# Hybrid encoder, one core: tile 0's index tables per piece, its four pieces routed in one run ahead of the first dots, projections of tiles 1 to 3 behind them

## The reference

```
h = h + even_layer(h)     # attention and a short convolution, joined, then @ even_w_out
h = h + peer_ffn(h)       # first expert block
h = h + odd_layer(h)      # pooling
h = h + peer_ffn(h)       # second expert block

def peer_ffn(x):          # per row; 8 heads, 128 + 128 sub-keys a head, 16 experts kept
    h = rms_norm(x, norm_g)
    q = h @ w_query                                  # 1024 -> 8 heads * 2 * 128
    s = q . sub_keys                                 # 2 lists of 128 scores a head
    sv, si = top_k(s, 16)
    top_s, pos = top_k(all 16 * 16 sums of sv, 16)   # two-step top 16 of 16384 experts
    idx  = expert numbers at pos                     # 128 a row
    gate = softmax(top_s)
    act  = gelu(expert_u[idx] . h)                   # 128 gathered rows of 1024, dotted
    return (gate * act) @ expert_v[idx]              # 128 more gathered rows, summed
```

## Time and profile before

| | |
|---|---|
| runs | 3245.25, 3246.49, 3247.8 us; median 3246.49 |
| the profiled execution | 3245.31 us, span 3243.3 us |
| busy over the span | PE 75%, DVE 69%, POOL 64%, ACT 16% |
| bytes moved | 1134.19 MB, 349 GB/s from HBM over the span |
| gathers | 2080, the first at 498.43 us, the last at 3226.14 us |

### The profile page before, as it was taken

How to read it: one execution, slowest core, us unless ns; L and a number is a source line. 1 busy time by engine, 2 the same in 40 slices (tenths; PEclk the granted TensorE clock), 3 DMA queues, 4 the chain that set the end, 5 groups by cost and what they waited for, 6 DMA issues and landing times.

```text
span 3243.3 us, 28912 instructions
## 1 busy us (share of the span) xinstructions
PE 2422.3 (75%) x5784; PEld 1036.3 (32%) x5784; DVE 2237.6 (69%) x5345; ACT 511.1 (16%) x1370; POOL 2073.7 (64%) x2147
## 2 busy tenths in 40 slices
PE   7999983886777667766678667867776777666667
PEld 3575341332223223322233233323332333222223
DVE  1123187798679866975699668976797679766663
ACT  1026211111111111111111111111111111111111
POOL 0000105777777777766777777777777777777776
PEclk9999996998899989988999899988999899998889
DMA  3121008999999999999999999999999999999999
GB/s 105 52 115 57 30 1 328 400 403 408 409 408 403 394 409 409 408 405 408 409 407 404 404 407 393 401 403 402 404 397 403 399 409 408 407 399 409 409 410 353
DMA packets 319926, 1134.19 MB, mean 350 GB/s; under 512 B 37824, under 2 KB 42944, under 8 KB 317792
## 3 DMA queue, kind: packets, MB, share of 16 engines
q0 software_dynamic: 299520, 1090.65, 85.0%
q1 hardware_dynamic: 20320, 42.62, 3.6%
HBM read 1130.97 MB, written 2.10 MB: 349 GB/s over the span
## 4 chain that ended last, share of the span: by engine, by line
PE 30%; DMA 23%; issue 18%; DVE 18%; POOL 7%; ACT 1%; DVEq 1%; SPq 0%; POOLq 0%; ACTq 0%
DMA v_ring<-in_peer_v,idx_v 18%; PE psum L1319 14%; DMA u_ring<-in_peer_u,idx_u 5%; DVE u_ring L1411 4%; POOL u_ring L1296 4%; PE psum L529 3%; POOL v_ring L1300 3%; PE psum L623 3%; PE psum L957 2%; PE psum L649 2%; DVE hres L1403 2%; PE psum L560 2%; DVE work L1082 1%; PE psum L989 1%; DVE si L1098 1%
## 5 line engine op out<-in xcount | busy, mean ns | idle before, releaser
L1319 PE MATMUL psum<-v_ring,w_col 128*128 128x512 f32 x3136 | 1700.6, 681 | 717.7 <-DMA v_ring<-in_peer_v,idx_v 636.2
L1411 DVE SCALAR_TENSOR_TENSOR u_ring<-u_ring,psum 128x1024 f32<-128x1024 f32 x1040 | 1256.4, 1216 | 541.0 <-DMA u_ring<-in_peer_u,idx_u 501.4
L1296 POOL DMA_INDIRECT u_ring<-in_peer_u,idx_u x1040 | 1018.6, 979 | 496.0 <-issue 264.3
L1300 POOL DMA_INDIRECT v_ring<-in_peer_v,idx_v x1040 | 1039.2, 999 | 318.1 <-issue 276.7
L1319 PEld LDWEIGHTS psum<-v_ring,w_col 128*128 128x128 f32 x3136 | 623.1, 214 | 1707.6 <-issue 1220.5
L1367 ACT ACTIVATE w_col<-ident,weight 128x128 f32<-128x128 f32 x768 | 291.5, 398 | 1248.0 <-PE psum L1319 1247.6
L1403 DVE SCALAR_TENSOR_TENSOR hres<-v_ring,weight,hres 128x1024 f32 (+1 forms) x256 | 328.3, 1282 | 40.3 <-DMA v_ring<-in_peer_v,idx_v 31.6
L957 PE MATMUL psum<-wq,hbT 128*128 (+1 forms) x512 | 249.8, 601 | 4.2 <-DVE work L1082 3.0
L452 POOL IOTA iota<- 128x16 f32 x1 | 0.1, 145 | 336.5 <-ACT catT L729 336.5
L957 PEld LDWEIGHTS psum<-wq,hbT 128*128 128x128 f32 x512 | 98.5, 194 | 130.6 <-issue 129.2
L529 PE MATMUL psum<-w_ring,hT 128*128 128x512 f32 (+1 forms) x240 | 106.1, 601 | 0.0
(11 more groups left out here) (222 smaller groups left out, 1492.4 us busy)
## 6 DMA issues: line engine op xcount, KB each, us to landing
u_ring<-in_peer_u,idx_u POOLq DMA_INDIRECT x1040, 8.2
v_ring<-in_peer_v,idx_v POOLq DMA_INDIRECT x1040, 8.1
wq<-in_peer_w_query SPq DMA_DIRECT2D x16, 1024.0 KB, 19.6
w_ring<-in_even_w_in SPq DMA_DIRECT2D x6, 2048.0 KB, 8.0
w_ring<-in_even_w_out SPq DMA_DIRECT2D x1, 4096.0 KB, 14.0
hres<-in_x SPq DMA_DIRECT2D x4, 512.0 KB, 5.2
out<-hres SPq DMA_DIRECT2D x1, 2048.0 KB, 6.6
hbT<-in_peer_sub_keys SPq DMA_DIRECT2D x6, 256.0 KB, 11.2
```

Of the source, the lines that this page charges most:

```text
L1296: nc.gpsimd.indirect_dma_start(u_ring[:, i % U_SLOTS, :], None, u_rows, bass.IndirectOffsetOnAxis(idx_u[par][:, i:i + 1], 0)).then_inc(s_u ...
L1300: nc.gpsimd.indirect_dma_start(v_ring[:, i % V_SLOTS, :], None, v_rows, bass.IndirectOffsetOnAxis(idx_v[par][:, i:i + 1], 0)).then_inc(s_v ...
L1319: ins = nc.tensor.matmul(y_ps[:, half, :], w_col[:, n % W_SLOTS, :], v_ring[:, i % V_SLOTS, 512 * half:512 * half + 512], start=False, sto ...
L1411: nc.vector.scalar_tensor_tensor(out=row, in0=row, scalar=1.0, in1=rows, op0=ALU.mult, op1=ALU.mult, accum_out=dot[par][:, i:i + 1]).then_ ...
```

## The change

- Tile 0's index table is written per piece (`piece_indices`), its logits with it; the exponentials (`piece_exponentials`) and gates (`piece_gates`) of the pieces are made later, the gates as hooks among the first three chunks of dots.
- The meta rows' indices are selected by PE and copied to `idxT` ahead of their gates (`meta_select_tensor`, `meta_indices_vector`, `meta_gates_vector`), the copied rows for their dots (`meta_rows_tensor`) are made earlier, and GpSimd starts chunk 0 without the wait for the projections; that wait stands before chunk 2.
- VectorE no longer adds projections 4 to 9. PE adds `hres` by a product with the identity in one bank (`LATE_BANK`) and ScalarE copies the sum back (`take_projected`). Half 4 and 5 stand around the meta selection, 6 to 9 between tile 0's pieces 1 and 2.
- All four pieces are routed before the first dot.
- `gather_pool` waits for the v slot behind the u gather rather than ahead of it. `w_col` has 12 slots for 4; `spread` and `sel` have room of their own; `u_ring` lies elsewhere; the scratch of GpSimd's gathers is 8192 bytes for the default.
- The transposes of tile 1's rows go into the sum of chunk 0 (behind its row 6), their norm behind the last dot of chunk 1.

```diff
-W_SLOTS = 4
+W_SLOTS = 12
...
         def project_tensor(pe, i):
             t, half = PROJECTED[i // 2], i % 2
+            c = slice(512 * half, 512 * half + 512)
+            dst = psum[0:rows_of(t), i, :] if i < 4 else LATE_BANK
             if i >= 4:
-                pe.wait_ge(s_mix, i - 3)
+                pe.wait_ge(s_mix, i)
+                nc.tensor.matmul(dst, ident[:, :], hres[:, t, c], start=True, stop=False)
             for k in range(KD):
...
+        def take_projected(act, i):
+            act.wait_ge(s_proj, i + 1)
+            t, half = PROJECTED[i // 2], i % 2
+            nc.scalar.copy(hres[:, t, 512 * half:512 * half + 512], LATE_BANK).then_inc(s_mix, 1)
...
+        def piece_indices(dve, s):
+            c = slice(2 * TOPK * s, 2 * TOPK * s + 2 * TOPK)
+            nc.vector.tensor_scalar(idxT[:, c], top_i[:, c], 0.0, None, ALU.add).then_inc(s_piece, 1)
...
+        def piece_gates(dve, s):
...
+            dve.wait_ge(s_pexp, s + 1)
...
         def gather_pool(pool, u, v, par):
...
-            if v is not None:
-                pool.wait_ge(s_idx_v, v + 1)
             for i in range(CHUNK):
                 if u is not None:
                     wait(pool, s_dot, CHUNK * u + i + 1 - U_SLOTS)
+                    apart(pool)
+                    nc.gpsimd.indirect_dma_start(u_ring[:, i % U_SLOTS, :], None, u_rows,
...
                 if v is not None:
+                    if i == 0:
+                        pool.wait_ge(s_idx_v, v + 1)
...
-            pool.wait_ge(s_proj, 2 * TILES)
             gather_pool(pool, 0, None, 0)
             gather_pool(pool, 1, None, 1)
+            pool.wait_ge(s_proj, 2 * TILES)
             gather_pool(pool, 2, 0, 0)
...
+            first_query(0)
+            take_projected(act, 4)
+            tail_scalar(act, 0, P, 2)
+            act.wait_ge(s_idx, 1)
+            stage_u(act, 0, 0)
+            take_projected(act, 5)
+            first_query(1)
+            act.wait_ge(s_piece, 1)
+            stage_u(act, 1, 1)
+            piece_exponentials(act, 0)
+            for i in range(6, 2 * TILES):
+                take_projected(act, i)
+            first_query(2)
+            piece_exponentials(act, 1)
+            first_query(3)
...
             logits_vector(dve, 0, P, 2)
+            meta_indices_vector(dve)
             gates_vector(dve, 0, P, 2)
...
+            for s in range(1, GROUPS):
+                for stage in topk_stages(dve, first_piece(1) + s, s, P):
+                    stage()
+                piece_indices(dve, s)
...
+            first_query(0)
+            project_tensor(pe, 4)
+            pe.wait_ge(s_routed, 2)
+            meta_select_tensor(pe, top_i, META_IDX, s_midx)
+            pe.wait_ge(s_gate, 1)
+            meta_select_tensor(pe, soft, META_GATE, s_gateT)
+            project_tensor(pe, 5)
+            pe.wait_ge(s_idx, 1)
+            pe.wait_ge(s_mgate, 1)
+            first_query(1)
+            for i in range(6, 2 * TILES):
                 project_tensor(pe, i)
+            first_query(2)
+            first_query(3)
...
-            experts_tensor(pe, 0)
+            experts_tensor(pe, 0, [(6, lambda: start_tensor(pe, 2, P, 0))])
...
-    nc = bacc.Bacc("TRN2", target_bir_lowering=False, num_devices=1)
+    nc = bacc.Bacc("TRN2", target_bir_lowering=False, num_devices=1, dynamic_dma_scratch_size=8192)
```

More of the change, by code:

```diff
@@ L645, in project_tensor @@
             t, half = PROJECTED[i // 2], i % 2
+            c = slice(512 * half, 512 * half + 512)
+            dst = psum[0:rows_of(t), i, :] if i < 4 else LATE_BANK
             if i >= 4:
-                pe.wait_ge(s_mix, i - 3)
+                pe.wait_ge(s_mix, i)
+                nc.tensor.matmul(dst, ident[:, :], hres[:, t, c], start=True, stop=False)
             for k in range(KD):
-                last = nc.tensor.matmul(psum[0:rows_of(t), i % 4, :], catT[:, k, cols_of(t)],
-                                        w_out_sb[:, k, 512 * half:512 * half + 512], start=(k == 0), stop=(k == KD - 1))
+                last = nc.tensor.matmul(dst, catT[:, k, cols_of(t)], w_out_sb[:, k, c], start=(i < 4 and k == 0), stop=(k == KD - 1))
             last.then_inc(s_proj, 1)
@@ L944, in start_tensor @@
                 pe.wait_ge(s_spread, GROUPS)
-            elif not isinstance(job, int) or job > 1:
+            elif isinstance(job, int) and job == 2:
+                pe.wait_ge(s_read, first_piece(2))
+            elif not isinstance(job, int) or job > 2:
                 pe.wait_ge(s_routed, first_piece(job) + 1)
@@ L980, in program @@
         META_BANKS = [psum[:, 4 + g, :] for g in range(GROUPS)]
[L981 removed]
+        META_Q = [u_ring[0:META, 4 + g, 0:512] for g in range(GROUPS)]
         metaT = q_T[:, :, :].rearrange("p a n -> p (a n)")[:, 0:LISTS * GROUPS * META]
@@ L1016, in meta_scalar, with meta_select_tensor, meta_indices_vector, meta_gates_vector @@
                 nc.scalar.copy(cand[32 * g:32 * g + META, :], META_BANKS[g][0:META, :]).then_inc(s_spread, 1)
-        def meta_tail_tensor(pe):
-            pe.wait_ge(s_gate, 1)
-            pe.wait_ge(s_setup, SETUP_STEPS)
[L1022 to L1035, removed]
+        META_IDX, META_GATE = QUERY_BANK[:, 0:TOPK], QUERY_BANK[:, TOPK:2 * TOPK]
+        def meta_select_tensor(pe, table, dst, done):
+            for e in range(2):
+                last = nc.tensor.matmul(dst, sel[:, e, :], table[:, TOPK * e:TOPK * e + TOPK], start=(e == 0), stop=(e == 1))
+            last.then_inc(done, 1)
+        def meta_indices_vector(dve):
+            dve.wait_ge(s_midx, 1)
+            nc.vector.tensor_scalar(idxT[:, cols(0)], META_IDX, 0.0, None, ALU.add).then_inc(s_idx, 1)
+        def meta_gates_vector(dve):
+            dve.wait_ge(s_gateT, 1)
+            nc.vector.tensor_copy(gateT[:, cols(0)], META_GATE).then_inc(s_mgate, 1)
+        def meta_rows_tensor(pe):
+            pe.wait_ge(s_setup, SETUP_STEPS)
             pe.wait_ge(s_hd, 1)
             for half in range(2):
-                last = nc.tensor.matmul(meta_rows[:, half, :], spread, meta_hf[:, 512 * half:512 * half + 512],
+                last = nc.tensor.matmul(meta_rows[:, half, :], spread[:, :], meta_hf[:, 512 * half:512 * half + 512],
                                         start=True, stop=True)
@@ L1712, in _, with first_query @@
             meta_scores_tensor(pe)
+            meta_rows_tensor(pe)
             start_tensor(pe, 1, P, 0)
             pe.wait_ge(s_hbT, 4)
-            query_tensor(pe, first_piece(1), 0, P, 0, KD, QUERY_BANK)
-            def piece(s, more=True):
+            def first_query(s):
+                query_tensor(pe, first_piece(1) + s, s, P, 0, KD, QUERY_BANK)
                 queryT_tensor(pe, first_piece(1) + s, P)
@@ L1721, in piece @@
                 scores_tensor(pe, first_piece(1) + s, s, P)
-                if more:
-                    query_tensor(pe, first_piece(1) + s + 1, s + 1, P, 0, KD, QUERY_BANK)
-            for s in range(PAIRS):
-                piece(s, more=s + 1 < PAIRS)
-                project_tensor(pe, 4 + s)
-                if s == 0:
-                    meta_tail_tensor(pe)
-            for i in range(4 + PAIRS, 2 * TILES):
+            first_query(0)
[9 more added lines that the diff above has]
+            for i in range(6, 2 * TILES):
                 project_tensor(pe, i)
+            first_query(2)
+            first_query(3)
             def pair(j, s, first=(), second=()):
```

135 lines of the change are left out of this document (76 added, 59 removed).

## The result

The changed kernel takes 3281.1 us (median of 4 runs, 3279.9 to 3282.4), the kernel before 3247.1 (3245.3 to 3249.1, 4 runs): ratio **1.0101**, interval 1.0089 to 1.0113, 34 us slower. Forecast was 3263, 16.5 us slower than the median of the kernel before, with a range that ended at 3277. The profiled execution closes without a rest: 3278.1 - 3243.3 = 34.8 us, of which gather 33 has 20.5 (564.54 against 544.05), the distance from gather 33 to the last 14.6 (2696.66 against 2682.09), and the tail -0.3.

What follows compares the result with a forecast made beforehand. GpSimd's gather queue was taken as the kernel's clock, so a late start shifts everything. Profiled 3245.3 + 19.5 (start) - 3 (stops) = 3261.8, hence 3263 us as median; range 3246 to 3277.

Steps and rivals of the forecast that it cites:

- The start: Up to gather 33: four late projections delay the first dot by 23.9 us to 531.1, gather 33 by 19.5 to 563.6.
- Behind gather 33: The gather stream after gather 33: chunk 0's sum and extra waits cost nothing, fewer stops win 3 us (0 to 8).
- the term of -3 us: Gather stream behind gather 33: split waits and twelve weight columns save 3 us of GpSimd's stops, range 0 to 8.
- the second wait and empty instruction: Ahead of each v gather on GpSimd: costs nothing; if additive at 0.05 us each, 52 us in all.
- chunk 0's sum: Chunk 0's sum, now with transposes in it: costs nothing, up to 5 us if ScalarE's stop at row 7 reaches GpSimd.
- the half ring: GpSimd's gather descriptors: half the room holds an estimated 512 descriptors, 56 gathers of nine, and costs nothing.
- The 3 us won on v slots: GpSimd's stops at full v slots in the stream: splitting the waits was taken to win 3 us, 0 to 8.
- More than the start: Rival, 9%: ScalarE's stop at chunk 0, an additive wait or a short descriptor queue brings the time to 3275 to 3315.
- ScalarE's stop at chunk 0: Mechanism in the 9% rival: ScalarE's stop at row 7 of chunk 0 reaches GpSimd, costed at up to 5 us.
- the additive wait: Mechanism in the 9% rival: the second wait ahead of each v gather adds 0.05 us, 52 us in all.
- the short queue: Mechanism in the 9% rival: GpSimd's gather descriptor queue runs short with half the scratch; no separate size given.

Runs made afterwards that it cites:

- e18: Changed kernel with projections 6 to 9 moved behind the scores of piece 3, no clears: 3257.9 us, ratio 1.0031.
- e16: Changed kernel with projections 6 to 9 behind the scores of piece 3 and 113 one-column VectorE clears before the meta routing: 3244.3 us, ratio 0.9989.
- e17: Kernel before with the stream's edits alone (split u and v waits, 12 weight columns, 8 KiB for gather descriptors): 3245.0 us, ratio 0.9995.
- e10: Changed kernel with 113 one-column VectorE clears in front of the meta rows' routing, which shift its later code: 3268.2 us, ratio 1.0056.
- e15: Kernel before with 5 one-column VectorE clears in front of the meta rows' routing: 3264.8 us, ratio 1.0052.
- e7: Kernel before with 5 one-column VectorE clears before the meta routing, run where the kernel before took 3619 to 3651 us: ratio 1.0027.
- e12: Kernel before with 5 one-column VectorE clears before the meta routing, repeated where the kernel before took 3619 to 3651 us: ratio 0.9981.

## Why the prediction was wrong

**The start was right.** First dot 531.85 for 531.1, gather 9 at 533.85 for 533.1, gather 33 at 564.54 for 563.6, VectorE idle 27.99 us ahead of piece 2 for 27.7, ended by TensorE. The products of two late projections begin 8.66 us apart, where I had 7.73 + 0.9 = 8.63. e18 and e16 show that these projections are the cause: with them behind piece 3 the first dot is at 503.4 and 502.4. Of 28 us at the first dot 25 reach gather 33 (from gather 9 to 33, e18 takes 34.4 us and the changed kernel 30.7). In e18 seven of the dots there wait for landings, 3.0 us in all, and in the changed kernel, whose ring was full, none; why they land late is open.

**The step that failed is "Behind gather 33"**, the term of -3 us; it measured +14.6, so the sum came out 18 us short. What failed in it is that VectorE's code was put at nothing, without a word: three stops of 6.65 us at a jump back to code that had to be fetched again, which moved the later gathers by 7.4, 4.8 and 5.5 us. The parts that I had priced were right or small: the second wait and empty instruction at 0, chunk 0's sum at 0 (the shift is 20.5 us at gather 33 and 20.7 at 905), the half ring at 0; e17 puts all of the stream's edits at 0.9985 to 1.0004. The 3 us won on v slots cannot be seen: GpSimd's idle beyond 0.30 us a gather, behind gather 33, is 41.4 us before, 39.4 in e10, 35.2 in e16 and 43.3 in e17, one execution each. What waited for TensorE's sums moved from the u gathers to the v gathers. Waits of GpSimd behind gather 33 (total, times, longest), kernel before, then changed kernel, where the first line carries the new stops:

```profile
POOL u_ring L1296 <- PE psum L1319: 42.2, 103, 6.2
...
POOL v_ring L1300 <- PE psum L1319: 20.1, 63, 1.2
```

```profile
POOL u_ring L1339 <- DVE u_ring L1462: 46.3, 78, 6.9
POOL v_ring L1351 <- PE psum L1370: 40.5, 104, 5.1
POOL u_ring L1339 <- PE psum L1370: 18.6, 57, 1.3
```

Missing was a term. I counted instructions that the change adds to an engine's stream as time, and asked what they wait for; that they also move the code behind them, 1200 us later, I did not ask. The page had a hint, the row of q14, and three stops of 6.3 us at outer loops' jumps in the trace before, with "issue" as their end. The rival "More than the start" covered the time, but by other mechanisms: the shift, 20.5 us at gather 33 and 20.7 at 905, rules out ScalarE's stop at chunk 0, and e17 the additive wait and the short queue. That its range holds the measured time is luck.

**Open.** A's core is shown both ways (e15 adds, e10 removes, the same stops and blocks). Where exactly an edge lies is fitted, not tested: between 1 and 2 records further on than in the kernel before. That the loop then touches a fourth block, and that this is why its start is no longer held, is inferred from its length, not seen. What makes the 3630 level is open too.

## What to carry to other kernels

Look at the row of instruction fetches and at VectorE's idle "issue" time behind jumps, before and after every edit: here five instructions far ahead of a loop of two and a half blocks had it fetched again, for 0.5% of the time, and of the change's 1% nearly half was code placement and not the edit. Compare an edit at a second code position before you judge it; a shorter inner loop may help as well, which no run here tried. And order an engine's work that nobody waits for behind the work that a chain waits for; here four projections between two queries cost 23 us.

## What the runs showed of the hardware

- A jump back to code that is then fetched again stops VectorE for 6.2 to 6.7 us at the 3250 level, at the new place with three packets of 8 KB about it. If nothing is fetched, the engine's idle at the same jump is 0.73 to 0.75 us.
- What such a stop costs the kernel depends on the gathers behind it: at the new jumps they drain to 22 GB/s and GpSimd stops for 4.5 to 6.9 us (changed kernel, e15, e18), at the first outer jump of the kernel before, with VectorE stopped for 6.36 us, it does not stop.
- VectorE with 113 small operations in a wait of 30.7 us loses nothing to them; e10 starts its first dot at 531.1, the changed kernel at 531.85.
- At the 3630 level 15 or 16 extra packets did not show in the time (e7, e12), though the stops are there (6.4, 5.4 and 5.0 us in e7). The core reads 315 GB/s over e7's span and 349 over that of the kernel before at the 3250 level. That slower transfers absorb a stop is a guess: after the first one in e7 GpSimd stood still for 9.7 us.
